# A two-layer MoE trunk on one core: ScalarE's queue loads the experts' rows

## The reference

```python
def hierarchical_moe(h, router_group, router_expert, w1, w3, w2):
    ...
    gates = g_gate * top_p / jnp.sum(top_p, axis=-1, keepdims=True)
    expert_idx = g_sel[:, None].astype(jnp.int32) * EXPERTS_PER_GROUP + top_i.astype(jnp.int32)
    return routed_experts(xf, expert_idx, gates, w1, w3, w2).reshape(b, t, d)

def expert_block(args):
    xb, e = args
    return (jax.nn.silu(xb @ w1[e]) * (xb @ w3[e])) @ w2[e]
```

## Time and profile before

| | us |
|---|---|
| median of 3 runs | 1859.63 |
| lowest, highest | 1856.82, 1860.03 |
| the profiled execution | 1855.57 |
| its span, first to last instruction | 1853.8 |
| mean granted TensorE clock | 0.957 |

### The profile page before, as it was taken

How to read it: one execution, slowest core, us unless ns; L and a number is a source line. 1 busy time by engine, 2 the same in 40 slices (tenths; PEclk the granted TensorE clock), 3 DMA queues, 4 the chain that set the end, 5 groups by cost and what they waited for, 6 DMA issues and landing times. The chain is left out here.

```text
span 1853.8 us, 27071 instructions
## 1 busy us (share of the span) xinstructions
PE 1658.8 (89%) x10664; PEld 888.4 (48%) x10793; DVE 1164.4 (63%) x1926; ACT 489.3 (26%) x854; POOL 182.9 (10%) x234
## 2 busy tenths in 40 slices
PE   6999889879969999999987999889689999999995
PEld 5766578744523333333332779554433333333332
DVE  5457977673336776766677533692437677666676
ACT  5254334353201111111112421572211111111112
POOL 2000724400100000000000000460100000000000
PEclk9999999988979999999998999999889999999997
DMA  6541000025669999999993220207669999999991
GB/s 171 149 119 35 6 3 4 3 92 221 256 246 422 421 421 419 421 421 420 421 417 145 91 91 23 92 1 300 247 260 421 420 422 421 420 422 420 420 407 59
DMA packets 117855, 471.41 MB, mean 254 GB/s; under 512 B 29152, under 2 KB 84448, under 8 KB 92128
## 3 DMA queue, kind: packets, MB, share of 16 engines
q1 hardware_dynamic: 115424, 461.26, 62.6%
q0 software_dynamic: 2304, 8.39, 1.1%
HBM read 452.85 MB, written 16.78 MB: 253 GB/s over the span
## 5 line engine op out<-in xcount | busy, mean ns | idle before, releaser
L783 DVE SCALAR_TENSOR_TENSOR x<-ps,gate_by_expert,x 128x512 f32<-128x512 f32 x512 | 348.4, 743 | 246.1 <-PE ps L733 245.9
L681 PE MATMUL ps<-w_unit,xT 128*48 128x512 f32 x1024 | 455.3, 598 | 37.8 <-DMA w_unit<-in_moe_w 31.6
L682 PE MATMUL ps<-w_unit,xT 128*48 128x512 f32 x1024 | 456.1, 599 | 0.0
L681 PEld LDWEIGHTS ps<-w_unit,xT 128*48 128x48 f32 x1024 | 124.6, 124 | 341.7 <-issue 339.7
L711 PE MATMUL ps<-w_unit,hidT 128*48 128x512 f32 x1024 | 249.1, 607 | 1.9 <-issue 1.9
L806 ACT ACTIVATE y_high_low<-y_cut 48x512 fp32r<-48x512 f32 x128 | 80.4, 628 | 421.4 <-DVE y_cut L754 418.9
L733 PE MATMUL ps<-y_high_low,slots_to_tokens 128*128 128x512 f32 x512 | 158.0, 430 | 14.4 <-DVE y_high_low L758 13.1
L733 PEld LDWEIGHTS ps<-y_high_low,slots_to_tokens 128*128 128x128 f32 x512 | 87.9, 192 | 132.6 <-issue 66.2
L1243 PE MATMUL ps<-hT_high,w_high 128*128 128x512 f32 (+1 forms) x344 | 139.8, 407 | 9.8 <-PE ps L1245 3.7
L1245 PE MATMUL ps<-hT_high,w_low 128*128 128x512 f32 (+1 forms) x344 | 136.0, 395 | 0.0
L1244 PE MATMUL ps<-hT_low,w_high 128*128 128x512 f32 (+1 forms) x344 | 135.7, 394 | 0.0
(11 more groups left out here) (368 smaller groups left out, 2187.1 us busy)
## 6 DMA issues: line engine op xcount, KB each, us to landing
w_unit<-in_moe_w SPq DMA_DIRECT2D x184, 2048.0 KB, 28.7
w_unit<-in_moe_w SPq DMA_DIRECT2D x16, 1024.0 KB, 24.2
x_rows<-sorted_rows SPq DMA_DIRECT2D x64, 192.0 KB, 28.4
w_unit<-in_od_w_qkv SPq DMA_DIRECT2D x12, 1024.0 KB, 5.5
w_raw<-in_ev_w_in SPq DMA_DIRECT2D x10, 1024.0 KB, 6.7
sorted_rows<-bias SPq DMA_DIRECT2D x32, 192.0 KB, 5.7
w_unit<-in_ev_w_out SPq DMA_DIRECT2D x2, 2048.0 KB, 11.1
w_unit<-in_od_w_out SPq DMA_DIRECT2D x2, 2048.0 KB, 10.4
```

What stands on the lines that cost most here:

```text
L681: nc.tensor.matmul(ps_1[0:MB, :], xT[b][:, k, :], w1[:, k, :], start=k == 0, stop=k == KD - 1)
L682: last = nc.tensor.matmul(ps_3[UP:UP + MB, :], xT[b][:, k, :], w3[:, k, :], start=k == 0, stop=k == KD - 1)
L783: nc.vector.scalar_tensor_tensor(out=xs, in0=ps_c[i % 4][:, :], scalar=gate(t), in1=xs, op0=ALU.mult, op1=ALU.add).then_inc(added, 1)
```

## The change

The row loads of experts 3 to 31 move from SP's list to ScalarE's. SP loses the wait for `xT_done` and the load; it still loads the rows of experts 0 to 2 and those of further blocks. ScalarE issues the rows of expert n+2 at the end of iteration n, behind `copy_hidden(n-1)`, after a wait that the rows of expert n-1 (the former content of the same slot) are turned. The loads keep their shape, slots and semaphores.

```diff
-    def load_rows(sp, j, row):
+    def load_rows(eng, j, row):
         rows = xrows[bass.ds(row, MB), :].rearrange("(i r) (k n) -> (r k) i n", i=XG, k=KD)
-        sp.dma_start(x_rows[j][:, :, :], rows).then_inc(rows_in[j], 16)
+        eng.dma_start(x_rows[j][:, :, :], rows).then_inc(rows_in[j], 16)
...
             for n in range(SLOTS, N_EXP):
-                sp.wait_ge(xT_done, n - SLOTS + 1)
-                load_rows(sp, slot(n), n * CAP)
                 if n in HALVED:
...
                 silu(act, n)
                 copy_hidden(act, n - 1)
+                if SLOTS <= n + 2 <= LAST:
+                    act.wait_ge(xT_done, n + 2 - SLOTS + 1)
+                    load_rows(act, slot(n + 2), (n + 2) * CAP)
             copy_hidden(act, LAST - 2)
```

## The result

The changed kernel takes 2006.18 us (median of 6 runs, 1999.57 to 2008.42) where the kernel before takes 1859.83 in the same comparison: 1.0777 times the time, with a 95% interval of 1.0761 to 1.0792. The forecast was 1935 with a range of 1885 to 1990. The direction and the mechanism came as forecast; the size did not, and the range was too narrow.

A forecast was written before the change was run, and what follows sets the result against it. The prediction took saturated weight transfers to bound the kernel, with TensorE's faster early pace only a loan. 1855.57 + 43 (rows waits, net) + 32 (clock) = 1930.6, with 4.1 from execution to median 1935 us; range 1885 to 1990.

The forecast's parts named there:

- What bounds the kernel before: Expert stages: transfers saturated near 420 GB/s, 15.4 us per expert; TensorE's early 14.0 us pace lives on weights landed ahead.
- The edits costed at nothing: SP losing 58 issues of 0.43 us gives 0; ScalarE's added wait and issue fit its 6.75 us idle: 0.
- The lead: Rows issued at h+1.2 (h: hidden activations turned), needed at h+14.64: 13.4 us, where they had two and a half periods.
- The duration of a load: Rows beside weights: 25 turns of 0.54 us, plus 0.3, 0.67 own data and 1.9 fixed: 16.3 us.
- The entry: Time from a load's issue to its first packet; forecast only within 1.9 us fixed, plus 0.3 for the packet under way.
- The alternation: TensorE waits for rows every second expert, 2.9 us then about 0: 14 long waits a layer, +43 us in all.
- The clock: TensorE's clock drops after long waits, 1.7 us each; two thirds of 28 waits taken: +32 us.
- (a): The forecast itself: 24 single turns per rows load, waits every second expert; 1935 us, from 1903 to 1996; chance 0.60.
- (b): Engine pauses let rows through at once, so pace falls back to the DMA's 15.38 us per expert: 1893 us; chance 0.16.
- (c): Several pieces per turn, or rows served first: load takes 5 us of 13.4, nobody waits; 1860 us; chance 0.14.
- (d): Rows out of the weight queue let the second half run at 14.7 instead of 15.38 us: 1841 us; chance 0.03.
- (e): ScalarE's load waits behind what SP already handed over, 22 us per load: +185, about 2045 us; chance 0.07.

The follow-up runs named there:

- e4_warm: Changed kernel with 70 small bf16 matmuls ahead of turn_rows in iterations 3, 5 to 27, keeping TensorE busy: 1947.49 us (1.0469 of the kernel before).
- e5_before_copy: Changed kernel with the rows load issued ahead of copy_hidden(n-1) instead of behind it: 1954.77 us (1.0524 of the kernel before).
- e2_long_runs: Changed kernel with each rows load read as 128 runs of 1536 bytes instead of 384 of 512: 1854.16 us (0.998 of the kernel before).
- e1_lead_two: Changed kernel with ScalarE loading rows one iteration earlier (expert n+3 instead of n+2): 1864.42 us (1.003 of the kernel before).
- e8: Kernel before, weight pieces 14 and 15 ahead of 13, rows in 1536-byte runs on SP's queue, transposes writing every third column: 1850.53 us (0.9948).
- e9: Changed kernel (rows on ScalarE's queue), weight pieces 14 and 15 ahead of 13, rows in 1536-byte runs, transposes writing every third column: 1851.02 us (0.9946).

## Why the prediction was right in kind and wrong in size

**What bounds the kernel before** held. Every version in which nobody waits for rows came out within about 2% of it, at the pace of its weights.

**The edits costed at nothing** held. ScalarE's issue takes 0.37 us and lies in idle time; SP's list without the rows brought nothing.

**The lead** held, and even a bit more of it was there: the issue goes out as the copy starts (741.01 beside 741.00), at h+0.7 instead of h+1.2. ScalarE's queue doesn't wait for the copy to end.

**The duration of a load** was the step that failed first. It was put at 16.3 us and is 17.9. The turns were right: 14.2 us forecast (25 x 0.54 and 0.67), 13.3 measured. The entry was wrong. I took that of idle engines, about 1.0 of the 1.9 us called fixed, and 0.3 for the packet under way; it is 3.5 us. With completion and the earlier issue this makes a wait of 4.0 instead of 2.9. That 17.9 also stands in the prediction, as the upper end of a load, is chance: there it came from 25 turns with a full weight packet each and the entry of idle engines; the turns were shorter and the entry longer than that. Ten of the 26 waits, three of them the first of the first layer, were longer still, near 6 us:

```profile
583.54 0.90 PE L669 MATMUL ps<-ident,x_rows 128*128 128x128 f32 x3 [6.31 <-DMA x_rows<-sorted_rows]
```

The entry of these loads is the same 3.5 us. Their data take 14.1 us instead of 13.4, and the last completion packet, which the slowest of the 16 engines sends, follows 1.6 to 2.3 us after the last piece instead of 0.6. Why one engine falls behind in these loads and not in the others is open. In all the waits sum to 129.6 us, 5.0 us each, where 28 x 2.9 = 81 were forecast: +91 net of the 38.3 us of waits for weights that vanished, in place of +43.

**The alternation** held: one long wait, one of nothing, 26 long waits where 28 were counted. The two at the end did not come.

**The clock** was the second step that was mis-sized. The form was right and its two terms were low. I let two thirds of the waits cost a drop, since 2.9 us lay between waits after which the clock stood and waits after which it fell. At 3.9 us and more all 26 cost one (the eight down matmuls behind each take 3.06 us or more): the down projections alone are busy for 42 us more (291.2 against 249.1), which is 26 times 1.6. And a drop cost about 2.3 us in all (59 over 26) instead of 1.7. The 1.7 counted eight down matmuls only; the three transposes ahead of them lose 0.35 us as well (0.90 instead of 0.55), and the last 0.2 to 0.3 us were not traced. Measured by e4_warm: 59 us in place of 32.

Together: 1855.6 + 91 + 59 = 2006, beside 2008.4 for the profiled execution of the changed kernel. The errors are not one. The size of the waits was off by the entry. The clock's share would have been too low even with waits of 2.9 us, since in e5_before_copy every wait of that length or more cost a drop; and the price of a drop was too low by itself. So even the upper end of (a), with waits of 4.5 us and a drop at each, came to 1996, and the range stopped at 1990.

**The rivals.** (b), that pauses regulate the pace down to 15.38 us, fell: the alternating pair puts the late load outside the pauses, as (b)'s own "against" had it. (c) needed several pieces per turn and fell with e2_long_runs. (d) fell: a second queue at the same run length took the rate nowhere (420 GB/s over 800 to 900 us in e1_lead_two, 422 in the kernel before); long runs raise it to 425, on either queue. (e) did not come either: the load passes the backlog of the other queue by turns. The sentence of the Trainium skill ("DMA: Bandwidth & Descriptors", section "Queues, rings and completion order") on round robin by packets agrees with the 397 beside 365 packets above; its typical 9 to 17 descriptors in a packet would have given (c), and the runs show one piece per turn. Of the same page's rule ("Rules for kernel authors") that spreading loads over issuing engines brings no bandwidth, e8 and e9 are the plainest case: 1850.5 and 1851.0 us.

## What to carry to other kernels

A small transfer that moves to a queue of its own doesn't pass a saturated queue for free: count its pieces per DMA engine, times the other queue's packet, plus the entry, and compare that with the lead from its issue to its use. Make its runs long, or issue it a period earlier; either alone came back to within 0.3% of the kernel before. Of the two the long runs leave more room: their loads land in 9.5 us of 13.9, where those with one more period took up to 25.1 of 28. And when a wait moves onto TensorE, price the clock with it, as a second cost that comes in the same places.

## What the runs showed of the hardware

- ScalarE's queue, starting beside SP's busy one, got its first packet through 3.5 us after the issue, 1.1 us on idle engines, whether the other queue's packets were of 16, 8 or 4 KB. About 1.4 MB passed in that time in each of these cases, but only 0.69 MB in 3.2 us where the weights had just begun.
- The queues of SP and ScalarE took turns one run for one, 512 bytes against 16 KB; the packets of a load of 24 runs per engine passed in 13.3 us (landing after 17.9), and a load of 8 runs landed after 9.5.
- Loads on ScalarE's queue that each need 14.2 us beside a full weight queue, issued every 14.0 us, line up: landing times of up to 25.1 us.
- The DMA issue of ScalarE went out when the copy ahead of it had started, not when it had ended.
- Weight pieces in one DMA with packets of 16 KB flowed at 420 GB/s, in two with 8 KB at 414, in four with 4 KB at 404.
- After waits of 2.0 to 2.6 us on TensorE the granted clock sometimes stood and sometimes fell to 0.50; after waits of 2.9 us or more it fell each time (e5_before_copy and the changed kernel).
